# Expert blocks that gather and scatter only their filled rows, and a combine step that reads plain tiles

## The reference

```python
group = top1(softmax(t @ w_group + b_group))              # 4 groups of 8 experts
e1, e2 = top2 of the group's 8 router logits              # two choices per token
gates = softmax over the two * p_group
y[token] += ((silu(x @ w_gate[e]) * (x @ w_up[e])) @ w_down[e]) * gate   # for both choices
```

## Time and profile before

| | |
|---|---|
| median of 3 runs | 3510.33 us (3510.32 to 3513.15) |
| the profiled execution's own time | 3513.74 us |
| its span | 3511.9 us |
| PE, DVE, ACT, POOL busy | 2972.1, 1971.5, 1518.9, 633.2 us |
| expert stage, layer 0 and 1 | about 1019 to 1631 us, 2834 to 3446 us |
| combine, layer 0 and 1 | 1632.66 to 1665.2 us, 3448.05 to 3481.7 us |

### The profile page before, as it was taken

One profiled execution on the slowest core, in us unless ns is written; L12 is line 12 of the kernel. 1 busy time (PEld: TensorE's weight loads), 2 busy tenths in 40 slices (PEclk: granted clock), 3 DMA queues, 4 the chain that ended last, 5 costly groups with the idle time before them and its releaser, 6 DMA issues. The chain is left out here.

```text
span 3511.9 us, 42490 instructions
## 1 busy us (share of the span) xinstructions
PE 2972.1 (85%) x13528; PEld 2263.7 (64%) x13528; DVE 1971.5 (56%) x2493; ACT 1518.9 (43%) x1704; POOL 633.2 (18%) x501
## 2 busy tenths in 40 slices
PE   3988888999759999995798999677699669999992
PEld 2433366765448777784787788466588557777771
DVE  3212454550258888886410455576644368888885
ACT  2001343440128888883311233232301148888882
POOL 1000000000011111111110445487600011111102
PEclk9999898999859999997599999887899679999996
DMA  4211410100329999996131232333220359999994
GB/s 174 78 56 35 128 35 28 36 18 0 122 91 386 397 399 396 398 397 237 41 107 53 82 93 92 129 106 106 72 96 31 121 210 395 396 399 398 397 392 167
DMA packets 302645, 640.45 MB, mean 182 GB/s; under 512 B 21616, under 2 KB 80112, under 8 KB 302448
## 3 DMA queue, kind: packets, MB, share of 16 engines
q1 hardware_dynamic: 263408, 513.73, 40.8%
q10 hardware_dynamic: 23040, 67.12, 4.8%
q0 software_dynamic: 16128, 58.73, 4.5%
HBM read 545.14 MB, written 94.37 MB: 182 GB/s over the span
## 5 line engine op out<-in xcount | busy, mean ns | idle before, releaser
L1884 DVE TENSOR_TENSOR moe_w_low<-moes_raw,moe_w_high 128x2048 fp32r<-128x2048 f32 x384 | 864.1, 2284 | 184.9 <-ACT moe_w_high L1811 184.9
L1811 ACT ACTIVATE moe_w_high<-moes_raw 128x2048 fp32r<-128x2048 f32 x384 | 720.4, 1920 | 98.6 <-PEq L162 67.1
L1705 POOL COPY moe_pick<-moes_tokens 128x1 int32 (+1 forms) x64 | 62.9, 983 | 1778.2 <-PE moe_px L1730 856.8
L186 PE MATMUL moe_py<-moe_w_high,moe_h_high 128*128 128x512 f32 x512 | 210.6, 411 | 0.0
L186 PE MATMUL moe_pg<-moe_w_high,moe_x_high 128*128 128x512 f32 x512 | 207.3, 405 | 0.0
L186 PE MATMUL moe_pu<-moe_w_high,moe_x_high 128*128 128x512 f32 x512 | 205.6, 402 | 0.0
L188 PE MATMUL moe_pg<-moe_w_high,moe_x_low 128*128 128x512 f32 x512 | 204.6, 400 | 0.0
L187 PE MATMUL moe_pg<-moe_w_low,moe_x_high 128*128 128x512 f32 x512 | 204.5, 399 | 0.0
L188 PE MATMUL moe_pu<-moe_w_high,moe_x_low 128*128 128x512 f32 x512 | 203.1, 397 | 0.0
L188 PE MATMUL moe_py<-moe_w_high,moe_h_low 128*128 128x512 f32 x512 | 203.1, 397 | 0.0
L187 PE MATMUL moe_pu<-moe_w_low,moe_x_high 128*128 128x512 f32 x512 | 202.9, 396 | 0.0
(11 more groups left out here) (367 smaller groups left out, 6308.2 us busy)
## 6 DMA issues: line engine op xcount, KB each, us to landing
moes_raw<-in_w_gate SPq DMA_DIRECT2D x128, 1024.0 KB, 7.4
moes_raw<-in_w_up SPq DMA_DIRECT2D x128, 1024.0 KB, 8.6
moes_raw<-in_w_down SPq DMA_DIRECT2D x128, 1024.0 KB, 7.3
Y<-moe_y ACTq DMA_DIRECT2D x64, 512.0 KB, 6.5
conv_raw<-in_w_in_ssd SPq DMA_DIRECT2D x24, 512.0 KB, 4.9
XC<-conv_c ACTq DMA_DIRECT2D x24, 512.0 KB, 2.9
Y<-B POOLq DMA_DIRECT2D x16, 512.0 KB, 12.2
HN<-norm_m_hn SPq DMA_DIRECT2D x16, 512.0 KB, 2.6
```

The source lines that it names most:

```text
L186: nc.tensor.matmul(out, lh, rh, start=start, stop=False)
L1705: nc.gpsimd.tensor_copy(pick[a][:, :], M.tokens[:, bass.ds(b, 1)]).then_inc(picked[a], 1)
L1811: nc.scalar.activation(wh[c % SPLIT_SLOTS][:, :], M.raw[j][:, :], ACT.Copy).then_inc(w_high, 1)
L1884: nc.vector.tensor_tensor(wl[j][:, :], M.raw[c % RAW_SLOTS][:, :], bits(wh[j][:, :]), ALU.subtract).then_inc(w_low, 1)
```

## The change

- **Router.** A filled place in `ptab` now holds 1 + token + 1024 * choice; an empty one holds 0. From that DVE makes `M.rows` (the row of the result, token + 1024 * choice) and `M.tokens` (the token); an empty place gets 8191 or more. `M.slot` and its two steps go.
- **Gather.** The indirect DMA gets a bound, so rows with an index past it are not fetched; POOL zeroes `xg` once at the start of the stage, since skipped rows keep what was there.
- **Store.** ACT no longer stores. POOL scatters each finished block by `M.rows` with a bound, into a `Y` of 2,048 rows ordered by choice and token. It does so in the same loop as the gathers: gather 0, gather 1, scatter 0, scatter 1. To start the count of `stored`, it writes a small unused tile twice.
- **Combine.** SP reads plain tiles of `Y`, with four buffers per choice instead of two.
- **Fill.** The zero fill of `Y` in `qk_stage` goes.

```diff
@@ qk_stage
-            nc.gpsimd.memset(zeros, 0.0).then_inc(zeroed, 1)
-            pool.wait_ge(zeroed, 1 + PRIMED)
-            for b in range(NE, NBLK):
-                pool.dma_start(K.Y[b * P:(b + 1) * P, :], zeros).then_inc(filled, 16)
@@ router_stage
-            step(V.scalar_tensor_tensor(out=expert[:, :], in0=where[:, :], scalar=float(P), in1=rank[:, :], op0=ALU.mult, op1=ALU.add))
-            step(V.tensor_copy(M.slot[:, :], expert[:, :]))
...
-            step(V.tensor_copy(M.tokens[:, 0:NBLK], ptab[:, :]))
+            step(V.tensor_scalar(late[:, :], ptab[:, :], 0.0, float(NO_ROW + 1), ALU.is_equal, ALU.mult))
+            step(V.scalar_tensor_tensor(out=late[:, :], in0=ptab[:, :], scalar=-1.0, in1=late[:, :], op0=ALU.add, op1=ALU.add))
+            step(V.tensor_copy(M.rows[:, :], late[:, :]))
+            step(V.tensor_scalar(second[:, :], ptab[:, :], float(S), -float(S), ALU.is_gt, ALU.mult))
+            step(V.tensor_tensor(late[:, :], late[:, :], second[:, :], ALU.add))
+            step(V.tensor_copy(M.tokens[:, 0:NBLK], late[:, :]))
@@ expert_stage, POOL
                 nc.gpsimd.indirect_dma_start(out=xg[a][:, :], out_offset=None, in_=K.HN[:, :],
-                                             in_offset=bass.IndirectOffsetOnAxis(ap=pick[a][:, :], axis=0)).then_inc(gathered[a], 16)
+                                             in_offset=bass.IndirectOffsetOnAxis(ap=pick[a][:, :], axis=0),
+                                             bounds_check=S - 1, oob_is_err=False).then_inc(gathered[a], 16)
+            def scatter(i, a):
+                pool.wait_ge(stored[a], i * 16 + 16)
+                nc.gpsimd.tensor_copy(back[a][:, :], M.rows[:, bass.ds(i * 2 + a, 1)]).then_inc(ready[a], 1)
+                pool.wait_ge(ready[a], i + 1 + PRIMED)
+                pool.wait_ge(y_kept, i * 2 + a + 1 + PRIMED)
+                nc.gpsimd.tensor_tensor(spare[:, 2 + a:3 + a], back[a][:, :], back[a][:, :], ALU.add)
+                nc.gpsimd.indirect_dma_start(out=Y[:, :], out_offset=bass.IndirectOffsetOnAxis(ap=back[a][:, :], axis=0),
+                                             in_=y[a][:, :], in_offset=None, bounds_check=2 * S - 1, oob_is_err=False).then_inc(stored[a], 16)
+            nc.gpsimd.memset(unused[:, :], 0).then_inc(cleared, 1)
+            for a in range(2):
+                nc.gpsimd.memset(xg[a][:, :], 0.0).then_inc(cleared, 1)
+            pool.wait_ge(cleared, 3)
+            for a in range(2):
+                pool.dma_start(K.unused[a * P:(a + 1) * P, :], unused[:, :]).then_inc(stored[a], 16)
             for a in range(2):
                 gather(a, a, 0)
             with pool.Fori(0, n) as i:
@@
                     gather(i * 2 + (2 + a), a, i + 1)
+                for a in range(2):
+                    scatter(i, a)
+            for a in range(2):
+                scatter(n, a)
@@ expert_stage, ACT
                 nc.scalar.activation(y[a][:, :], py[a][:, :], ACT.Copy).then_inc(y_kept, 1)
-                act.wait_ge(y_kept, i * 2 + a + 1 + PRIMED)
-                act.dma_start(Y[bass.ds((i * 2 + a) * P, P), :], y[a][:, :]).then_inc(stored[a], 16)
@@ combine_stage
-                    if t >= 2:
-                        pool.wait_ge(added[k], t - 1)
-                    c = k * NT + t
-                    nc.gpsimd.indirect_dma_start(out=rows[k][t % 2][:, :], out_offset=None, in_=K.Y[:, :],
-                                                 in_offset=bass.IndirectOffsetOnAxis(ap=M.slot[:, c:c + 1], axis=0)).then_inc(got[k][t % 2], 16)
+                    if t >= RING:
+                        sp.wait_ge(added[k], t - RING + 1)
+                    r = k * S + t * P
+                    sp.dma_start(rows[k][t % RING][:, :], K.Y[r:r + P, :]).then_inc(got[k][t % RING], 16)
```

More of the change, by code:

```diff
@@ L54 @@
 MAGIC = 1.5 * 2.0 ** 23
+NO_ROW = 8191
 PIECE = D * DE // P // 2
@@ L83 @@
 C_TOK = C_IOTA + P
-C_FA = C_TOK + NT
+C_FA = C_TOK + 2 * NT
 C_FB = C_FA + 1
@@ L117, in constants @@
     c[:, C_IOTA:C_IOTA + P] = i
-    c[:, C_TOK:C_TOK + NT] = q + P * np.arange(NT)[None, :]
+    c[:, C_TOK:C_TOK + 2 * NT] = q + P * np.arange(2 * NT)[None, :] + 1
     def frequencies(rot):
@@ L371, in qk_stage @@
                                    ("w_loaded", "projected", "raw_ready", "turned", "rope_steps", "stored"))
-        zeroed, filled = st.sem("zeroed"), st.sem("filled", primed=False)
         block = st.primed_block()
@@ L1509, in router_stage @@
         planf = st.sb("planf", [P, 1 + NBLK])
+        late, second = st.sb("late", [P, NBLK]), st.sb("second", [P, NBLK])
         row1 = [st.sb(f"row1{a}", [P, P]) for a in range(2)]
@@ L1633, in _ @@
                 V.tensor_scalar(row1[n % 2][:, :], C[:, C_IOTA:C_IOTA + P], rank[:, n:n + 1], None, ALU.is_equal).then_inc(onehot, 1)
-                V.tensor_scalar(col1[n % 2][:, :], C[:, C_IOTA:C_IOTA + NBLK], where[:, n:n + 1], C[:, C_TOK + n % NT:C_TOK + n % NT + 1],
+                V.tensor_scalar(col1[n % 2][:, :], C[:, C_IOTA:C_IOTA + NBLK], where[:, n:n + 1], C[:, C_TOK + n:C_TOK + n + 1],
                                 ALU.is_equal, ALU.mult).then_inc(onehot, 1)
-            step(V.memset(M.tokens[:, NBLK:], 0))
+            step(V.memset(M.tokens[:, NBLK:], NO_ROW))
             dve.wait_ge(placed, T2)
-            step(V.tensor_copy(M.tokens[:, 0:NBLK], ptab[:, :]))
+            step(V.tensor_scalar(late[:, :], ptab[:, :], 0.0, float(NO_ROW + 1), ALU.is_equal, ALU.mult))
[4 more added lines that the diff above has]
+            step(V.tensor_copy(M.tokens[:, 0:NBLK], late[:, :]))
 def expert_stage(nc, K, A, layer, M):
@@ L1650, in expert_stage @@
         wh, wl = ([st.sb(f"{n}{j}", [P, PIECE], F32R) for j in range(SPLIT_SLOTS)] for n in ("w_high", "w_low"))
-        pick = [st.sb(f"pick{a}", [P, 1], I32) for a in range(2)]
-        spare = st.sb("spare", [P, 2], I32)
+        pick, back = ([st.sb(f"{n}{a}", [P, 1], I32) for a in range(2)] for n in ("pick", "back"))
+        spare, unused = st.sb("spare", [P, 4], I32), st.sb("unused", [P, 4], I32)
         xg = [st.sb(f"xg{a}", [P, D]) for a in range(2)]
@@ L1665, in expert_stage @@
         gathered = [st.sem(f"gathered{a}", primed=False) for a in range(2)]
-        picked, stored = ([st.sem(f"{n}{a}") for a in range(2)] for n in ("picked", "stored"))
+        stored = [st.sem(f"stored{a}", primed=False) for a in range(2)]
+        picked, ready = ([st.sem(f"{n}{a}") for a in range(2)] for n in ("picked", "back_ready"))
+        cleared = st.sem("cleared", primed=False)
         block = st.primed_block()
@@ L1800, in _ @@
             for a in range(2):
-                pe.wait_ge(stored[a], n * 16 + 16 + PRIMED)
+                pe.wait_ge(stored[a], n * 16 + 32)
         @block.scalar
@@ L1830, in keep_y @@
                 act.wait_ge(w_used, i * PIECES + (2 * a + 10) + PRIMED)
-                act.wait_ge(stored[a], i * 16 + PRIMED)
+                act.wait_ge(stored[a], i * 16 + 16)
                 nc.scalar.activation(y[a][:, :], py[a][:, :], ACT.Copy).then_inc(y_kept, 1)
-                act.wait_ge(y_kept, i * 2 + a + 1 + PRIMED)
-                act.dma_start(Y[bass.ds((i * 2 + a) * P, P), :], y[a][:, :]).then_inc(stored[a], 16)
             def round_(i, more):
@@ L1941, in combine_stage, with _ @@
 def combine_stage(nc, K, layer, M):
+    RING = 4
     with Stage(nc, f"comb{layer}") as st:
-        rows = [[st.sb(f"rows{k}{a}", [P, D]) for a in range(2)] for k in range(2)]
-        got = [[st.sem(f"got{k}{a}") for a in range(2)] for k in range(2)]
+        rows = [[st.sb(f"rows{k}{a}", [P, D]) for a in range(RING)] for k in range(2)]
+        got = [[st.sem(f"got{k}{a}") for a in range(RING)] for k in range(2)]
         added = [st.sem(f"added{k}") for k in range(2)]
         block = st.ctx.enter_context(nc.Block())
-        @block.gpsimd
-        def _(pool):
+        @block.sync
+        def _(sp):
             for t in range(NT):
                 for k in range(2):
-                    if t >= 2:
-                        pool.wait_ge(added[k], t - 1)
-                    c = k * NT + t
-                    nc.gpsimd.indirect_dma_start(out=rows[k][t % 2][:, :], out_offset=None, in_=K.Y[:, :],
-                                                 in_offset=bass.IndirectOffsetOnAxis(ap=M.slot[:, c:c + 1], axis=0)).then_inc(got[k][t % 2], 16)
+                    if t >= RING:
+                        sp.wait_ge(added[k], t - RING + 1)
+                    r = k * S + t * P
+                    sp.dma_start(rows[k][t % RING][:, :], K.Y[r:r + P, :]).then_inc(got[k][t % RING], 16)
         @block.vector
@@ L1962, in _ @@
                 for k in range(2):
-                    dve.wait_ge(got[k][t % 2], 16 * (t // 2 + 1))
+                    dve.wait_ge(got[k][t % RING], 16 * (t // RING + 1))
                     if k:
                         dve.wait_ge(added[0], t + 1)
-                    nc.vector.scalar_tensor_tensor(out=K.X[:, t, :], in0=rows[k][t % 2][:, :], scalar=M.weight[:, k, t:t + 1],
```

(9 more changed lines are left out.)

5 lines of the change are left out of this document (removed).

## The result

| | before | after |
|---|---|---|
| median | 3510.32 us | 3594.05 us (3591.35 to 3602.03, 4 runs) |
| ratio | | 1.024, interval 1.0224 to 1.0256 |
| span of the profiled execution | 3511.9 us | 3589.6 us |
| bytes over the span | 640.45 MB | 598.55 MB |

The account below looks back on a forecast made before the run. It took PE, not DMA, to bound the round. Loop +82, start +11, end +4, router +1 and combine -15 summed to +83 us: span 3595, median 3593 us, range 3510 to 3660.

Parts of the forecast that it names:

- loop: Expert stage's rounds: the late gather stalls `turn_x` 14 times a layer, 28 in all, +2.95 us each: +82 us.
- start: Expert stage's start: memsets, small DMAs and DVE's splits delay the fourth `turn_x` by 4 to 7.3 us, taken 5.5; two layers +11.
- end: Expert stage's end: POOL addition, DMA instruction and slower start replace ACT's store; about +2 us (0.5 to 3), twice: +4.
- combine: Combine: plain loads with four buffers take 25 to 27 us instead of 32.5; -6 to -8.5 a layer, -15 in all.
- outside the mixtures: Router's extra small steps, +0.6 us a layer, twice: +1; the removed fill 0.
- The bytes: Gather and store in the rounds: 1 MB of 14.7 a round goes, worth nothing by itself since no one waits for bytes.
- ACT's stores: Round's end: ACT and DVE come 0.7 us earlier, so the wait of `turn_h` may go, -0.55 us a round.
- POOL's queue: Gather 0 behind scatter 1: instruction held by one split, over at 1304.6, lands 6.7 us later, PE stalls 3.5 us.
- the short stall: Rival: gather slips in (stall 1.2 us, 3529) or is held once and lands sooner (1.9, 3547); chance 0.16.
- The period: Stalled round in the expert stage: 36.4 + 3.5 = 39.9 us against 36.95, +2.95.
- Router and fill: Router: two steps go, five come behind the last small matmul, +0.6 us a layer; fill is covered by PE's products, 0.
- The landing: Half a gather under load: 6.7 us after its instruction taken, bounds 3.4 and 6.7; the skill's figure gives 2.6.

Follow-up runs that it names:

- experiment 5: Changed kernel with a round's two gathers issued ahead of the previous round's scatters, plus all 128 rows gathered with no bound on the gather: 3490.48 us, 0.9939 to before.
- experiment 1: Changed kernel with the two gathers of a round issued ahead of the scatters of the round before it: 3487.96 us, ratio to before 0.9932.
- the last experiment: Changed kernel with gathers ahead of scatters, plus two unused 32-byte tiles giving load buffers and split weights the addresses of the kernel before: 3490.42 us, 0.9947.
- experiment 3: Changed kernel with an unbounded gather of all 128 rows, empty places reading the last token's row, one more router step: 3557.18 us in one run.
- experiment 6: Changed kernel with gathers ahead of scatters, DVE zeroing `xg` instead of POOL, first gathers ahead of POOL's unused-tile writes: 3482.2 us, ratio 0.9923.

## Why the prediction was right

It forecast 3593 us; 3594.05 was measured, by the mechanism that it named. That the two agree to 1 us is luck. The sum is of parts that were each off by some us:

| both layers | said | measured |
|---|---|---|
| loop, from the fourth `turn_x` to the last copy of y | +82 | +81.9 |
| start | +11 | +14.7 |
| end | +4 | +6.5 |
| combine | -15 | -16.7 |
| outside the mixtures | +1 | -8.7 |
| span | +83 | +77.7 |

The profiled run of the changed kernel was 2.7 us under the median of its runs and that of the kernel before 3.4 over, so the medians differ by 83.7.

- **The bytes.** Said: worth nothing. Right for the gather: experiment 5. The store's half has only experiment 1's 374 GB/s against 397, with PE busy for 492.71 of 500 us.
- **ACT's stores.** Said: the 0.55 us wait of `turn_h` goes. Right in the changed kernel, and nearly so in the last experiment (3.4 us of PEld and PE from 1080 to 1600, against 16.6 before). With the gathers first and the closer spacing it stayed (18.6 us); that PE runs ahead of DVE there is my reading and was not tested.
- **POOL's queue.** Said: from the start of ACT's copy (1296.69) to the end of the gather's instruction 7.9 us, held by one split. Measured 7.5, held by one split. Said: lands 6.7 later; measured 6.2 in the median. Said: stall 3.5; measured 3.0 to 4.0, mean 3.2 (distance of two starts less 0.23; the profile's idle time is 2.8 to 3.8). The scatter's addition was held once before, as said. Of the rivals, the short stall was the nearest, but not within the 0.3 us that I named: instructions with a bound were held when they started 0.09 and 0.14 us ahead of a split, and not at 0.17, so this one would have had to start some 0.4 us earlier. Slipping in also gave less than the 2.3 us that I priced: in experiment 3 the stall fell by 0.8.
- **The period.** Said +2.95 a round. Measured between gathers 0, as the mean of 13: 40.1 us in layer 0 and 40.0 in layer 1, against 36.95. But the terms differ: -0.55 for `turn_h`, +3.2 for the stall, +1.1 for the lower clock (10 of 14 times 1.6), -0.7 for the closer spacing. The sum names neither of the last two, and the two rounds a layer that do not stall are shorter than before; that the loop came out at +82 is these misses cancelling.
- **The start.** Said +5.5 a layer, at most +7.3. Measured +7.7 in layer 0 (+7.0 in layer 1) from the stage's first instruction to the fourth `turn_x` (24.4 us against 16.7). The first DMA instruction was held as said (1023.05, 2.96 us) and was over only at 1026.01, but the landing took 6.9 us more, longer than the 3.4 to 6.7 that I had between.
- **The end.** Said +2 a layer. Measured +3.2: 9.1 us from ACT's copy to the combine's first load, against 5.8.
- **The combine.** Said -7.5 a layer. Measured -8.1 and -8.5.
- **Router and fill.** Said +0.6 a layer and 0. The steps behind the last small matmul run from 1011.58 to 1012.96, 1.4 us where one cast took 0.2; less the two steps that went, 0.2 us each, that is +0.8. The 64 products that covered the fill took 29.68 us after and 29.46 before: 0.
- **Outside.** From the table, the mixtures cost 45.7 + 40.7 = 86.4 us. The first starts 2.8 earlier and "between" is 5.6 shorter: 86.4 - 8.4 = 78, the difference of the spans is 77.7. Of the 5.6, some 5 lie in the state-space scan, which the diff does not touch. That is no scatter of one profile: the scan takes 299.5 to 302.2 us in all eight kernels with the change and 304.2 to 306.1 in all four without. I made no experiment on its cause, so some 4 to 5 us of what the reordered kernels gain are not explained.
- **The landing.** The Trainium skill (DMA: Bandwidth & Descriptors, Anatomy of one DMA) would have half a gather land in an estimated 2.6 us; measured 6.2 under load, so the trace does not agree with it there. Only at the stage's start, before the loads are dense again, did gathers with a bound land in 3.1 and 3.2 us behind the instruction (those issued at 1037.82 and 1042.97).

## What to carry to other kernels

Before work is moved to an engine with slack, look at what stands behind it in that engine's order: here POOL was busy for 83.62 of 500 us, and a scatter that waits for the end of a round was put ahead of a gather that opens the next. Issue the early-needed transfer first and let the late one wait behind it; that one reordering turned +2.4% into -0.7%. And price a stall of a few us on TensorE by more than its length, because the clock may fall behind it: here 1.1 us a round on top of 3.2.

## What the runs showed of the hardware

- After stalls of about 3 us the granted clock was 0.50 for some 3 us, with products 0.43 us apart, behind 10 of 14 stalls of 3.0 to 4.0 us, and behind 5 of 14 of 1.8 to 3.0 us (experiment 3).
- In the steady stretch an indirect DMA instruction with a bound started 0.53 us behind a POOL addition of 0.19 us, one without 0.15 us. Behind an addition that a split had held for 1.28 us the one with a bound, too, started after 0.15 us (the scatter at 1124.05): the bound's 0.4 us hides behind a held operation.
- POOL's indirect DMA instruction, not only its small operations, is held by a DVE operation on two SBUF operands: 2.93 us where DVE began 0.29 us before it. Where DVE began behind it, one without a bound was not held at 0.08 to 0.11 us (0.99 us, experiment 3); of those with a bound the ones at 0.09 and 0.14 us were held (3.38 and 3.31 us, experiment 6) and those at 0.17 us were not (1.05 us, the changed kernel).
- In the loop half a block's rows land 6.2 to 6.5 us behind the instruction. The gather 1 of all rows lands after 6.7 us, against 6.5 for half. The first row's packet of gather 0 moved at 1131.96, 2.9 us behind its instruction: most of the landing is not bytes.
